# Two heads alternate matmul by matmul in the attentions and the index of a two-block transformer kernel

## The reference, cut to what matters

```
# block 1: stick-breaking attention, 16 heads of dimension 64, query blocks of 128 tokens
z = q k^T * 64**-0.5                      # each query against the keys up to its block
log_1m_beta = where(mask, log_sigmoid(-z), 0)
after = reverse_cumsum(log_1m_beta) - log_1m_beta
a = where(mask, exp(log_sigmoid(z) + after), 0);  out = a v
# block 2: index of 8 heads of dimension 32, and attention of 8 heads of dimension 64
score = sum_h w_h * relu(q_idx_h k_idx^T * 32**-0.5)      # the largest 128 keys of a query are kept
logits = q k^T * 64**-0.5 + rel_bias;  p = softmax(logits over the kept keys);  out = p v
```

## Time and profile before

| | before |
|---|---|
| median of three runs | 2154.19 us (2154.13 to 2160.44) |
| the profiled execution | 2163.67 us, its span 2161.5 us |
| TensorE busy | 2051.0 us, 95% of the span |
| VectorE, ScalarE, GpSimd busy | 886.9, 718.7, 499.9 us |
| mean granted TensorE clock | 0.97 of 2.4 GHz |

### The profile page before, as it was taken

How to read it: one execution, slowest core, us unless ns; L and a number is a source line. 1 busy time by engine, 2 the same in 40 slices (tenths; PEclk the granted TensorE clock), 3 DMA queues, 4 the chain that set the end, 5 groups by cost and what they waited for, 6 DMA issues and landing times.

```text
span 2161.5 us, 21967 instructions
## 1 busy us (share of the span) xinstructions
PE 2051.0 (95%) x8901; PEld 1565.3 (72%) x8901; DVE 886.9 (41%) x1445; ACT 718.7 (33%) x1032; POOL 499.9 (23%) x268
## 2 busy tenths in 40 slices
PE   2899999999999999997999999989899999999998
PEld 2666666787878786786888888856675577888886
DVE  6675757210303122323333333437734544433433
ACT  3444446323323232233222222313234442222223
POOL 0322222453545353341000000223224511100000
PEclk9999999999999999998999999979998999999999
DMA  7432222332222221321322322452111122323321
GB/s 240 151 99 77 98 78 79 118 126 78 78 79 77 78 93 64 117 79 59 98 83 93 98 90 73 117 83 83 59 49 59 30 69 78 98 97 98 96 83 56
DMA packets 175114, 192.20 MB, mean 89 GB/s; under 512 B 9570, under 2 KB 158344, under 8 KB 174888
## 3 DMA queue, kind: packets, MB, share of 16 engines
q1 hardware_dynamic: 170952, 180.76, 26.0%
q10 hardware_dynamic: 3632, 7.70, 1.7%
q0 software_dynamic: 432, 2.36, 0.3%
HBM read 186.09 MB, written 4.72 MB: 88 GB/s over the span
## 4 chain that ended last, share of the span: by engine, by line
PE 50%; DVE 2%; ACTq 1%; ACT 1%; issue 0%; POOL 0%; DVEq 0%; POOLq 0%
PE bank L1229 13%; PE bank L1230 12%; PE bank L1232 12%; PE bank L1250 2%; PE bank L1251 2%; PE bank L1249 2%; PE bank L1458 1%; PE bank L1398 1%; PE bank L1476 1%; ACTq L2193 1%; PE bank L1373 1%; PE bank L1465 0%; PE bank L1356 0%; PE bank L1259 0%; DVE SW L1815 0%
## 5 line engine op out<-in xcount | busy, mean ns | idle before, releaser
L2335 POOL TENSOR_TENSOR wl<-stg,wh 128x1024 fp32r<-128x1024 f32 x156 | 376.3, 2413 | 1054.9 <-ACT wh L1985 1054.3
L1229 PE MATMUL bank<-hH,wh 128*128 128x512 f32 x1344 | 568.4, 423 | 28.0 <-POOL hL L2328 9.9
L1230 PE MATMUL bank<-hL,wh 128*128 128x512 f32 x1344 | 540.2, 402 | 0.0
L1232 PE MATMUL bank<-hH,wl 128*128 128x512 f32 x1344 | 539.7, 402 | 0.0
L1985 ACT ACTIVATE wh<-stg 128x1024 fp32r<-128x1024 f32 (+2 forms) x298 | 304.4, 1023 | 321.5 <-PE bank L1232 224.0
L1229 PEld LDWEIGHTS bank<-hH,wh 128*128 128x128 f32 x1344 | 257.3, 191 | 139.3 <-issue 77.6
L1232 PEld LDWEIGHTS bank<-hH,wl 128*128 128x128 f32 x1344 | 257.8, 192 | 62.9
L1230 PEld LDWEIGHTS bank<-hL,wh 128*128 128x128 f32 x1344 | 258.9, 193 | 50.1 <-issue 0.7
L1521 DVE TENSOR_TENSOR wl<-stg,wh 128x1024 fp32r<-128x1024 f32 (+2 forms) x142 | 168.9, 1190 | 247.7 <-ACT wh L1985 247.4
L1229 PE MATMUL bank<-h2H,wh 128*128 128x512 f32 x352 | 140.8, 400 | 0.0
L1232 PE MATMUL bank<-h2H,wl 128*128 128x512 f32 x352 | 140.0, 398 | 0.0
(11 more groups left out here) (286 smaller groups left out, 2770.0 us busy)
## 6 DMA issues: line engine op xcount, KB each, us to landing
stg<-in_w_in SPq DMA_DIRECT2D x57, 1024.0 KB, 5.1
stg<-in_w_ada SPq DMA_DIRECT2D x24, 1024.0 KB, 5.2
stg<-in_w_ffn_in SPq DMA_DIRECT2D x22, 1024.0 KB, 5.1
stg<-in_w_ffn_gate SPq DMA_DIRECT2D x11, 1024.0 KB, 5.3
stg<-in_w_ffn_up SPq DMA_DIRECT2D x11, 1024.0 KB, 5.2
stg<-in_w_ffn_down SPq DMA_DIRECT2D x10, 1024.0 KB, 5.0
stg<-in_w_proj_ret SPq DMA_DIRECT2D x8, 1024.0 KB, 5.0
stg<-in_w_out SPq DMA_DIRECT2D x8, 1024.0 KB, 5.0
```

The costliest lines, as they stand in the source:

```text
L1229: T.matmul(ps, wh, xh, start=j["first"] and k == 0, stop=False)
L1230: T.matmul(ps, wh, xl, start=False, stop=False)
L1232: t = T.matmul(ps, wl, xh, start=False, stop=j["stop"] and last)
L2335: G.tensor_tensor(lo, src, hi, ALU.subtract).then_inc(s["w_lo_pool"], 1)
```

## The change

In `attend`, the five tiles' scores become three groups (`SECS`: key blocks 1 and 3, then 2, then 0). A group takes both banks of ring Z, one for each head, and its matmuls alternate between the heads; `sbz_first` is gone. VectorE empties each head's bank to the same tiles as before (tile 0 in two halves), and ScalarE's part is a step of its own (`sba`) in the order of `SOFT`: tiles 1 and 2, then 0, then 3 and 4. `sbsp` follows in that order. `sbo` becomes one step of eight matmuls, the two heads in turn. In `select`, two heads' index matmuls stand together in both Z banks, and a yield comes after two heads: 4 + 16 + 1 yields for each i. In `attn` an item is a pair of heads (16 items), with six logits tiles (the sixth is KI's), probabilities in TMP 0, 1, 4, 5, four bias tiles (two of them QI's), a lag of three items in place of six, `at` still head after head, and `av` in turn; the rates are 0.65 and 1.0 in place of 1.2 and 1.8. The arithmetic is the same. Cut to its core:

```diff
+SECS = [[(1, 0), (3, 384)], [(2, 0)], [(0, 0)]]
+SOFT = [(1, 2), (0,), (3, 4)]
-ITEMS = [(hh, i) for hh in range(8) for i in range(4)]
+ITEMS = [(pr, i) for pr in range(4) for i in range(4)]
@@ attend
-        for n in range(5):
-            take("Z", ("sbz", pr, n))
-            emit("sbz", pr, n)
-            give(("sbz", pr, n))
-            yield
-            if n > 1:
-                emit("sbsp", pr, n - 2)
-            yield
-        yield
+        for g in range(3):
+            for hh in range(2):
+                take("Z", ("sbz", pr, g, hh))
+            emit("sbz", pr, g)
+            for hh in range(2):
+                give(("sbz", pr, g, hh))
+            yield
+            for n in SOFT[g]:
+                emit("sba", pr, n)
+                yield
+            for n in SOFT[g - 1] if g else ():
+                emit("sbsp", pr, n)
+                yield
...
-        for hh in range(2):
-            emit("sbo", pr, hh)
-            yield
+        emit("sbo", pr)
+        yield
+        yield
@@ select
                 if hh < 8:
-                    take("Z", ("idx", i, hh))
+                    if hh % 2 == 0:
+                        while p.busy & set(p.RINGS["Z"]):
+                            yield
+                        for e in range(2):
+                            take("Z", ("idx", i, hh + e))
+                        emit("idx2", i, hh)
                     emit("idx", i, hh)
                     give(("idx", i, hh))
                 if hh:
                     emit("score", i, hh - 1)
-                yield
+                if hh % 2:
+                    yield
@@ attn
-        for n in range(len(ITEMS) + 6):
-            for lag, step in enumerate((last, copied, turned, lambda n: emit("as", n), lambda n: emit("ae", n), greatest, logits)):
-                m = n - 6 + lag
-                if 0 <= m < len(ITEMS):
-                    step(m)
+        for n in range(len(ITEMS) + 3):
+            for lag, step in ((2, lambda n: emit("as", n)), (1, greatest), (0, logits), (1, lambda n: emit("ae", n)), (3, last),
+                              (2, turned), (2, copied)):
+                if 0 <= n - lag < len(ITEMS):
+                    step(n - lag)
                     if step in (logits, turned, last):
                         yield
-    stage(1.2)
+    stage(0.65)
-    for k0, rate in ((4, 1.8), (0, 0)):
+    for k0, rate in ((4, 1.0), (0, 0)):
@@ tensor: sbz, sbo, idx2, al, av
+                zb = [free(pe, ("sbz", pr, g, hh)) for hh in range(2)]
+                for e, (j, off) in enumerate(SECS[g]):
                     w = S - P * j
-                    if m == 2 and e:
-                        pe.wait_ge("sbz_first", pr + 1)
+                    for hh in range(2):
+                        t = T.matmul(zb[hh][:, off:off + w], kt[64 * hh:64 * hh + 64, j * P:(j + 1) * P],
+                                     qt[64 * hh:64 * hh + 64, j * P:S], start=True, stop=True)
...
                 for j in range(4):
-                    n, off = WHERE[hh, j]
                     w = S - P * j
+                    for hh in range(2):
+                        n, off = WHERE[hh, j]
+                        t = T.matmul(ob[64 * hh:64 * hh + 64, j * P:S], vt[:, j * P + 64 * hh:j * P + 64 * hh + 64],
+                                     ZS[n][:, off:off + w], start=j == 0, stop=j == 3)
...
+                for e in range(2):
+                    hh, r0 = h0 + e, 32 * ((h0 + e) % 4)
+                    T.matmul(zb[e][:, 0:w], QI[r0:r0 + 32, hh // 4, i * P:(i + 1) * P], KI[r0:r0 + 32, 0:w],
+                             start=True, stop=True).then_inc(fill(("idx", i, hh)), 1)
...
+                for hh in range(2):
+                    lo = 64 * hh
+                    T.matmul(zb[hh][:, 0:w], QA[lo:lo + 64, pr, i * P:(i + 1) * P], KA[lo:lo + 64, pr, 0:w],
+                             start=True, stop=True).then_inc(fill(("al", n, hh)), 1)
...
                 for c in range(i + 1):
+                    for hh in range(2):
+                        lo = 64 * hh
+                        t = T.matmul(ob[lo:lo + 64, i * P:(i + 1) * P], VA[:, c, pr * P + lo:pr * P + lo + 64],
+                                     pt_of(n, hh)[:, c * P:(c + 1) * P], start=c == 0, stop=c == i)
```

More of the change, by code:

```diff
@@ L812, in logits @@
         def logits(n):
[L813 to L816, removed]
+            pr, i = ITEMS[n]
+            if i == 0 and pr + 1 < 4:
+                for hh in range(2):
+                    emit("bias_row", 2 * pr + 2 + hh)
+            for hh in range(2):
+                take("Z", ("al", n, hh))
             emit("al", n)
@@ L820, in greatest @@
             emit("ag", n)
-            give(("al", n))
+            for hh in range(2):
+                give(("al", n, hh))
         def turned(n):
-            take("C", ("at", n))
+            for hh in range(2):
+                take("C", ("at", n, hh))
             emit("at", n)
@@ L828, in copied @@
             emit("ac", n)
[L829 to L835 removed]
+            for hh in range(2):
+                give(("at", n, hh))
+        for hh in range(2):
+            emit("bias_row", hh)
+        for n in range(len(ITEMS) + 3):
[3 more added lines that the diff above has]
+                    step(n - lag)
                     if step in (logits, turned, last):
@@ L1270, in sbz @@
                 emptied(pe, of_job("sbk", pr))
-                zb = free(pe, ("sbz", pr, n))
-                for e, (hh, j, off) in enumerate(secs):
+                zb = [free(pe, ("sbz", pr, g, hh)) for hh in range(2)]
+                for e, (j, off) in enumerate(SECS[g]):
                     w = S - P * j
-                    if m == 2 and e:
-                        pe.wait_ge("sbz_first", pr + 1)
-                    t = T.matmul(zb[:, off:off + w], kt[64 * hh:64 * hh + 64, j * P:(j + 1) * P],
-                                 qt[64 * hh:64 * hh + 64, j * P:S], start=True, stop=True)
-                    if m == 2 and not e:
-                        t.then_inc(s["sbz_first"], 1)
-                t.then_inc(fill(("sbz", pr, n)), 1)
+                    for hh in range(2):
+                        t = T.matmul(zb[hh][:, off:off + w], kt[64 * hh:64 * hh + 64, j * P:(j + 1) * P],
+                                     qt[64 * hh:64 * hh + 64, j * P:S], start=True, stop=True)
+                        if e == len(SECS[g]) - 1:
+                            t.then_inc(fill(("sbz", pr, g, hh)), 1)
             def sbc(pr, n):
@@ L1396, in idx @@
                 emptied(pe, of_job("fm", "KI", 0))
-                zb = free(pe, ("idx", i, hh))
-                T.matmul(zb[:, 0:w], QI[r0:r0 + 32, hh // 4, i * P:(i + 1) * P], KI[r0:r0 + 32, 0:w],
-                         start=True, stop=True).then_inc(fill(("idx", i, hh)), 1)
+                zb = [free(pe, ("idx", i, h0 + e)) for e in range(2)]
+                for e in range(2):
+                    hh, r0 = h0 + e, 32 * ((h0 + e) % 4)
+                    T.matmul(zb[e][:, 0:w], QI[r0:r0 + 32, hh // 4, i * P:(i + 1) * P], KI[r0:r0 + 32, 0:w],
+                             start=True, stop=True).then_inc(fill(("idx", i, hh)), 1)
             def ga(r):
@@ L1468, in av @@
+            def at_(n):
+                for hh in range(2):
+                    pe.wait_ge("v_as", 4 * n + 2 * hh + 2)
+                    cb = free(pe, ("at", n, hh))
+                    for c in range(ITEMS[n][1] + 1):
+                        t = T.transpose(cb[:, c * P:(c + 1) * P], lg_of(n, hh)[:, c * P:(c + 1) * P], ident[:, :])
+                    t.then_inc(fill(("at", n, hh)), 1)
             def av(n):
-                hh, i = ITEMS[n]
-                pr, lo = hh // 2, 64 * (hh % 2)
+                pr, i = ITEMS[n]
```

172 lines of the change are left out of this document (93 added, 79 removed).

## The result

The changed kernel takes 2119.55 us (median of 4 runs, 2117.67 to 2120.43) beside 2154.22 us of the kernel before on the same chip: a ratio of 0.9831, 95% interval 0.9812 to 0.9850. It is faster by 34.7 us where 84 were forecast, and lies outside the range. The profiled execution has a span of 2117.4 us.

What follows compares the result with a forecast made beforehand. TensorE, busy 2051.0 of 2161.5 us, was taken as the bound. Saving 106 us less waits of 10, 8 and 4 gave 84 us, so 2154.2 to 2070 us (chance 0.72, own range 2050 to 2090, full range 2046 to 2110).

Steps and rivals of the forecast that it cites:

- What the change saves on TensorE: All edited parts: alternating two heads halves the matmul streams and saves blocks of 0.40 us each; with turns 106 us.
- second and third rival: Second: row tiles 128 columns wide don't overlap, 2093 us, chance 0.06; third: pair takes 1.3 times one head, 2088 us, 0.08.
- What is late next: Three places where TensorE comes sooner to steps waiting for VectorE: first attention 10 us, selection 8 us, second attention 4 us.
- the terms of 10, 8 and 4 us: Waits taken off the gain: first cumulative matmul of a pair 10 us, selection 8 us, second attention 4 us.
- one chain, that to the first cumulative matmul: First attention: emptyings, ScalarE's instructions and sbsp take 10.1 us, 12.1 with three others, against 11.7 us; wait taken as 10.
- the slower rival: First attention: each pair waits 6 us more, then runs at 1.2 GHz (7 us more); 104 us, 2164 us, chance 0.02.
- My upper bound, all of 29 us: Selection: waits on VectorE cost between 0 and all that index and turns give, 29 us; 8 us was taken.
- the drain: Linear attention's last head, 13.0 us without products, would end among products: 8 us gained, plus 5 us for the slow start.
- 65% at most: Second attention: lasting some 90 us, VectorE, ScalarE and GpSimd are 65% busy at most; waits 0 to 10 us, 4 taken.
- the 105 that I had called wrong: Sign: the second attention should last some 90 us; over 105 us would show the forecast wrong.
- The first rival: First attention's scores and selection: VectorE and ScalarE become the bound; only 46.5 us gained, 2108 us, chance 0.11.
- a low clock for over 60 us in all: Sign for the whole kernel: a low clock for more than 60 us in all would show the forecast wrong.

Runs made afterwards that it cites:

- e1: Kernel before with the change in the first attention alone (scores and value products): 2127.30 us, ratio to before 0.9886.
- e2: Kernel before with the change in the index and its turns alone: 2152.21 us, ratio to before 1.0000.
- e3: Kernel before with the change in the second attention alone: 2144.31 us, ratio to before 0.9965.
- e13: Changed kernel with seven of eight adaptive-sum instructions cut to 2 columns in place of 256: 2099.66 us, ratio to before 0.9738.
- e4: Changed kernel with adaptive sums and value transposes moved from ring Z to a bank of ring C: 2123.56 us, ratio to before 0.9875.
- e12: e9 with VectorE adding an item's logits before scaling the item before it, in the second attention: 2090.88 us, ratio to before 0.9701.
- e9: Changed kernel with three more turns a pair before the first cumulative matmul of the first attention: 2104.25 us, ratio to before 0.9771.
- e5: Changed kernel with the second attention's steps reordered, VectorE's sums first and logits matmuls last in a round: 2123.14 us, ratio to before 0.9858.
- e6: Changed kernel with a turn after each index head again, the pairs kept: 2119.19 us, ratio to before 0.9841.
- e8: Changed kernel with four more turns a pair before the first cumulative matmul of the first attention: 2111.66 us, ratio to before 0.9802.
- e10: Changed kernel with the weights' low parts made by VectorE instead of GpSimd while the two attentions run: 2138.03 us, ratio to before 0.9929.

## Why the prediction was wrong

**What the change saves on TensorE** was right. Forecast were 93 us of streams and blocks; TensorE's busy time fell by 79.7. Part of what is missing is the index, 9.8 us less in place of 16: more of it now runs at 1.2 GHz (763 ns an instruction in place of 628). Rows of 128 columns overlap as the 64x64 tiles of the earlier trace rows do, so the second and third rival fell: a pair takes 1.01 times one head (1.13 for 1.12 us), not 1.3. The Trainium skill (TensorE: Matmul & The Clock Gate, "Measured speedup vs the span model") has 3.07 times the speed for four row tiles, 77% of ideal; for two, this trace shows no such loss.

**The step that failed is "What is late next"**, the terms of 10, 8 and 4 us. e1, e2 and e3 measure each part with its waits: 24.6, 0 and 7.5 us by ratio, where the forecast has 46.8 - 10 = 37, 29 - 8 = 21 and 29.9 - 4 = 26. So the waits with what follows them are 22, 29 and 22 us, in place of 22 together. Each failed in its own way:

- *First attention.* Waits grew by 19 us (19.8 and 4.2 for the emptyings, 5.1 at L1309, less the 10.2 of before), where I had 10. I checked one chain, that to the first cumulative matmul, found 10.1 us of it for 11.7 us of room, and it did fit: L1309 waits less than before. I did not look at the step that stands right behind the third scores, the adaptive sum, which in every second pair needs a Z bank. "Three turns, 2.1 us of products, cover the 1.4 us" of emptyings counts only the emptyings; what stands ahead of them in the queue was 4.6 us in the example above. e13 shows that this is what decides. I also left out the clock: I priced 1.2 GHz only in the slower rival. Behind each of the four waits products start 0.43 us apart for 4.4 us (273.4 to 277.8 in the example), so that a wait of 5.3 us costs over 7.
- *Selection.* My upper bound, all of 29 us, is what happened. "VectorE is idle for 20 of the 25 us before 1450, and that fills first" held: from its first weighted score to its last selection step VectorE takes 105 us in after (1400.5 to 1505.0) and took 141 before. But that is VectorE's gain. TensorE, in the same stretch and with 15 turns less, waits at the index (7.6 us, none before) and at the transposes (7.8 us for 4.3), and has the lower clock; what the vanished drain gives is then all that is left to pay for it. I had the row for it (1.36 us a step where a turn lasts 0.83) and counted the turns once as a gain at the drain, not a second time as cover taken from the selection.
- *Second attention.* "65% at most" of each engine is an average again. Two banks taken by one item, where two items had one each, make the logits wait for the sums of the item before; they stood behind a scaling. It lasted 106 us, over the 105 that I had called wrong.

**The first rival**, VectorE and ScalarE as the bound, 2108 us, is nearest, and even it was too low, since it left 25.9 us in the second attention and 20.3 in the value products. The Trainium skill's rule (TensorEngine Tiling (Array Packing), "PSUM Bottleneck"), that tiling does not speed up the emptying of PSUM, was the rule against the change, and the traces bear it out in its result. They add what kind of bottleneck it is: not the emptying's speed (1.28 us in a wait of 5.32), and not the bank (e4), but the place of the emptying in VectorE's queue (e12, e13) and the products beside it (e9).

**The drain** went as forecast: no 13 us without products before the second attention; the product matmuls gain some 18 us there in place of 13 (before's own slow stretch taken off), part of which is work that now lies earlier.

**The slower rival** decides from a long wait in each pair. Four of eight pairs have one, of 5 us with 4.4 us of low clock behind it, some 29 us together by the figures above: its mechanism is there, at about a quarter of its 104 us. The sign "a low clock for over 60 us in all" could tell nothing: with 0.970 granted of 2161.5 us and two levels only, before itself has some 130 us at 1.2 GHz; after has 150.

What stays open: the share of the low clock in the lost 49 us was not measured by itself, since no run changes the clock without the waits. An estimate from the clock records: TensorE is busy at 1.2 GHz for 95 us in before and 106 in after, worth 6 us, and up to 15 if before's two longer stretches are taken off. The selection was not tried with VectorE's chain cut shorter. And in the second attention the pairs of heads, the lag of three items and the rates of 0.65 and 1.0 came in together; no run separates them.

## What to carry to other kernels

When TensorE gets faster, take the room that it leaves to each step that needs a bank or an operand from another engine, all of them and not only the one that waits today, and lay against it what stands ahead in that engine's queue at that moment; an engine at 70% on average is the bound there. Where a wait shows up, moving it to another bank or to the next step gains nothing (e4, e5, e6); either put what frees the bank ahead in the queue (e12, some 14 us for a changed order in a list) or put work beside it, as much as the stage has and no more (e9 against e8, by their traces). Both together, with the change, give 2090.88 us, ratio 0.9701 (0.9671 to 0.9731), some 64 us where the change alone gives 36 by its ratio.

## What the runs showed of the hardware

Two float32 matmuls of 128 columns' width on other rows of the array (32 or 64 deep) run fully at the same time over 512 columns: 1.13 us for both, 1.12 for one, starts 7 ns apart. The 0.40 us for a block of small tiles, worked out from the earlier trace rows, stays with two heads.

A wait of TensorE of 5.32 us is followed by products at 0.43 us a matmul, 1.2 GHz, for the next 4.4 us; a wait of 1.19 us is not (1656.65 us: the products behind it start 0.23 us apart). Whether several short waits cost less than one long one of the same sum is not shown: e4, with 8 waits of 25.2 us and longest 4.3, ended no faster than the changed kernel.

While GpSimd subtracts a 128x1024 weight (2.34 us at 268.97, 2.80 at 1637.60), VectorE's instruction of 0.4 to 0.8 us that starts beside it lasts 2.52 and 2.38 us, in both attentions (269.07 and 1638.30 us above). Over the first attention's stage it costs VectorE some 20 us, which is less than the 24 us that VectorE needs to make those low parts itself (e10).
